# Two landing tiles for each expert weight piece, one buffer for the split down weights, and another order of the splits

## The reference, cut to what matters

```
dest = ...                      # tokens sorted by expert, in blocks of 128 rows
def expert_block(args):
    xblk, e = args              # xblk: 128 x 1024
    hid = jax.nn.silu(xblk @ w_gate[e]) * (xblk @ w_up[e])     # 1024 x 256 each
    return hid @ w_down[e]                                     # 256 x 1024
yb = lax.map(expert_block, (xb, block_e))
```

## Time and profile before

| | us |
|---|---|
| median of 3 runs | 3005.43 (3005.19 to 3011.29) |
| the profiled execution | 3002.1 |
| its span | 3000.5 |
| PE busy in the span | 2580.1 (86%) |
| DVE busy | 1809.9 (60%) |
| ACT busy | 1250.2 (42%) |
| POOL busy | 657.2 (22%) |

### The profile page before, as it was taken

The page is one execution under the profiler, slowest core; times in us unless marked ns, Lnnn a source line. Parts: engine busy times, 40 slices in busy tenths (PEclk is TensorE's granted clock), DMA queues, the critical chain, the costliest instruction groups (busy, mean ns, idle before and its releaser), DMA issues. The chain is left out here.

```text
span 3000.5 us, 42077 instructions
## 1 busy us (share of the span) xinstructions
PE 2580.1 (86%) x12607; PEld 2079.5 (69%) x12608; DVE 1809.9 (60%) x2274; ACT 1250.2 (42%) x1486; POOL 657.2 (22%) x718
## 2 busy tenths in 40 slices
PE   7989998998998999979977843998989989998956
PEld 6778777777877877747856732777777767776832
DVE  3346887787788655537445714566656676566427
ACT  3343453454245333335221102566656665556400
POOL 2012112221212111100002073233323323223200
PEclk9999999999999999989988966999999999999978
DMA  5323233221322232164543135677778797779367
GB/s 120 63 46 68 57 49 59 58 56 50 78 57 50 65 80 75 60 207 138 164 149 102 55 85 178 241 278 276 248 264 280 278 319 261 258 260 326 132 264 316
DMA packets 246835, 462.84 MB, mean 154 GB/s; under 512 B 27144, under 2 KB 151560, under 8 KB 244686
## 3 DMA queue, kind: packets, MB, share of 16 engines
q1 hardware_dynamic: 211870, 377.44, 41.2%
q0 software_dynamic: 34864, 84.04, 7.5%
HBM read 401.02 MB, written 94.40 MB: 165 GB/s over the span
## 5 line engine op out<-in xcount | busy, mean ns | idle before, releaser
L59 PE MATMUL dn_pj<-x_hi,dn_hi 128*128 128x512 f32 x1024 | 439.6, 429 | 3.1 <-PEq L84 1.8
L61 PE MATMUL dn_pj<-x_hi,dn_lo 128*128 128x512 f32 x1024 | 411.7, 402 | 0.0
L60 PE MATMUL dn_pj<-x_lo,dn_hi 128*128 128x512 f32 x1024 | 410.7, 401 | 0.0
L1008 DVE SCALAR_TENSOR_TENSOR uc_half<-u_in,par,uc_half 128x512 f32<-128x512 f32 x480 | 383.3, 799 | 13.1
L2303 ACT ACTIVATE e_hi<-e_raw 128x2048 f32 (+1 forms) x128 | 244.7, 1913 | 244.2 <-DMA e_raw<-in_w_up_e_dram 244.2
L2363 DVE TENSOR_TENSOR e_lo<-e_raw,e_hi 128x2048 f32 (+1 forms) x128 | 290.4, 2287 | 51.5 <-ACT e_hi L2303 51.2
L59 PE MATMUL gu_ps<-e_hi,xg_hi 128*128 (+1 forms) x752 | 310.4, 413 | 0.0
L2200 POOL DMA_INDIRECT y_rows<-y_block,idx_scatter x98 | 160.5, 1637 | 626.0 <-ACT y_block L2322 514.0
L61 PE MATMUL gu_ps<-e_hi,xg_lo 128*128 (+1 forms) x752 | 294.3, 391 | 0.0
L60 PE MATMUL gu_ps<-e_lo,xg_hi 128*128 (+1 forms) x752 | 293.5, 390 | 0.0
L1147 POOL TENSOR_TENSOR a_lvl<-a_t,lvl_mask 128x512 f32<-128x512 f32 x112 | 167.8, 1515 | 352.2 <-PE dn_a L686 223.5
(11 more groups left out here) (374 smaller groups left out, 5010.7 us busy)
## 6 DMA issues: line engine op xcount, KB each, us to landing
e_raw<-in_w_gate_e_dram SPq DMA_DIRECT2D x128, 512.0 KB
e_raw<-in_w_up_e_dram SPq DMA_DIRECT2D x128, 512.0 KB
e_raw<-in_w_down_e_dram SPq DMA_DIRECT2D x128, 512.0 KB
dn_raw<-in_w_in_dram SPq DMA_DIRECT2D x64, 512.0 KB
y_rows<-y_rows SPq DMA_DIRECT2D x8, 2560.0 KB, 31.5
y_rows<-y_rows SPq DMA_DIRECT2D x8, 1536.0 KB, 26.2
gate_rows<-qkv_next SPq DMA_DIRECT2D x16, 512.0 KB, 3.2
br_raw<-in_w_oa_dram SPq DMA_DIRECT2D x16, 512.0 KB
```

The costliest lines, as they stand in the source:

```text
L59: nc.tensor.matmul(out, w_hi, x_hi, start=first, stop=False)
L60: nc.tensor.matmul(out, w_hi, x_lo, start=False, stop=False)
L61: return nc.tensor.matmul(out, w_lo, x_hi, start=False, stop=last)
L1008: ins = stt(out=uc[:], in0=u_in[:, t:t + HALF], scalar=w, in1=uc[:], op0=ALU.mult, op1=ALU.add)
```

## The change

Each landing tile gets a second half, taken by the parity of the expert. The load of expert e into a half waits until expert e-2's piece has been read. Because the two halves share one arrival semaphore, SP also waits until the previous expert's piece has arrived before it issues the next. SP's order becomes gate/up of e+2, then down of e. The split down weights get one buffer in place of two. In an expert's first block ScalarE makes the high part of the down weights last, after the output copy, and VectorE the low part last; VectorE makes the low part of hidden first and puts gate/up piece 0 of e+2 ahead of the product.

```
@@ -2067,11 +2067,11 @@
         with ExitStack() as ctx:
             GU = 2
             BUFS = 3
-            raw = [sb(ctx, f"e_raw{i}", [P, 2, 4 * FF]) for i in range(GU + 1)]
+            raw = [sb(ctx, f"e_raw{i}", [P, 2, 2, 4 * FF]) for i in range(GU + 1)]
             wh = sb(ctx, "e_hi", [P, BUFS, KT, 2, FF], F32R)
             wl = sb(ctx, "e_lo", [P, BUFS, KT, 2, FF], F32R)
-            dh = sb(ctx, "ed_hi", [P, 2, 2, D], F32R)
-            dl = sb(ctx, "ed_lo", [P, 2, 2, D], F32R)
+            dh = sb(ctx, "ed_hi", [P, 2, D], F32R)
+            dl = sb(ctx, "ed_lo", [P, 2, D], F32R)
             xg = [sb(ctx, f"x_gather{s}", [P, D]) for s in range(2)]
             xh = sb(ctx, "xg_hi", [P, 2, KT, P], F32R)
             xl = sb(ctx, "xg_lo", [P, 2, KT, P], F32R)
@@ -2112,8 +2112,8 @@
                         j = e % BUFS
                         x = w[:, j] if isinstance(j, int) else w[:, bass.ds(j, 1)].rearrange("p o k w f -> p (o k) w f")
                         return x[:, 4 * i:4 * i + 4, :, :].rearrange("p k w f -> p w k f")
-                    return raw[i][:].rearrange("p w (k f) -> p w k f", k=4), wkf(wh), wkf(wl)
-                return raw[i][:], of(dh, odd(e)), of(dl, odd(e))
+                    return of(raw[i], odd(e)).rearrange("p w (k f) -> p w k f", k=4), wkf(wh), wkf(wl)
+                return of(raw[i], odd(e)), dh[:], dl[:]
 
             def plan(eng, e):
 
@@ -2143,30 +2143,45 @@
 
             @block.sync
             def _(sp):
-                def load_gate_up(e, first):
+                def arrived(e, i):
+                    if not isinstance(e, int) or e > 0:
+                        sp.wait_ge(w_in[i], e * 32)
+                        alone(sp, self.passed)
+
+                def into(e, i, n):
+                    return of(raw[i], odd(e))[:, n, :]
+
+                def load_gate_up(e):
 
                     for i in range(GU):
-                        if not first:
-                            sp.wait_ge(lo_s, e * GU + (i + 1 - GU))
+                        arrived(e, i)
+                        if not isinstance(e, int) or e >= 2:
+                            sp.wait_ge(lo_s, e * GU + (i + 1 - 2 * GU))
+                        alone(sp, self.passed)
                         for n, w in enumerate((a["w_gate_e"], a["w_up_e"])):
                             src = w[0, bass.ds(e, 1)].rearrange("o (p k) f -> p (o k) f", k=KT)[:, 4 * i:4 * i + 4, :]
-                            sp.dma_start(raw[i][:, n, :].rearrange("p (k f) -> p k f", k=4), src).then_inc(w_in[i], 16)
-
-                def load_down(e, first):
-
-                    if not first:
-                        sp.wait_ge(dlo_s, e)
+                            sp.dma_start(into(e, i, n).rearrange("p (k f) -> p k f", k=4), src).then_inc(w_in[i], 16)
+
+                def load_down(e):
+
+                    arrived(e, GU)
+                    if not isinstance(e, int) or e >= 2:
+                        sp.wait_ge(dlo_s, e - 1)
+                    alone(sp, self.passed)
                     for n in range(2):
                         src = a["w_down_e"][0, bass.ds(e, 1)].rearrange("o (c p) n -> p (o c) n", p=P)[:, n, :]
-                        sp.dma_start(raw[GU][:, n, :], src).then_inc(w_in[GU], 16)
-
-                load_gate_up(0, True)
-                load_down(0, True)
-                load_gate_up(1, False)
-                with sp.Fori(2, E) as e:
-                    load_gate_up(e, False)
-                    load_down(e - 1, False)
-                load_down(E - 1, False)
+                        sp.dma_start(into(e, GU, n), src).then_inc(w_in[GU], 16)
+
+                load_gate_up(0)
+                load_gate_up(1)
+                for e in range(2):
+                    load_gate_up(e + 2)
+                    load_down(e)
+                with sp.Fori(2, E - 2) as e:
+                    load_gate_up(e + 2)
+                    load_down(e)
+                for e in range(E - 2, E):
+                    load_down(e)
 
             @block.gpsimd
             def _(pool):
@@ -2245,11 +2260,10 @@
                         last = nc.tensor.transpose(ht[:, s, h, :], hid[:, s, h * P:(h + 1) * P], self.ident[:])
                     last.then_inc(ht_done, 1)
 
-                def down(e, s):
-                    j = odd(e)
+                def down(s):
                     for h in range(2):
                         for hf in range(2):
-                            w = lambda x: x[:, bass.ds(j, 1), h, hf * HALF:(hf + 1) * HALF].rearrange("p o b -> p (o b)")
+                            w = lambda x: x[:, h, hf * HALF:(hf + 1) * HALF]
                             last = split3(nc, yp[:, hf, :], hh[:, s, h, :], hl[:, s, h, :], w(dh), w(dl), h == 0, h == 1)
                     last.then_inc(y_done, 1)
 
@@ -2272,7 +2286,7 @@
                         pe.wait_ge(hl_s, n)
                         pe.wait_ge(dlo_s, e_prev + 1)
                         pe.wait_ge(y_ready, n + LAG - 1)
-                        down(e_prev, 1 - s)
+                        down(1 - s)
 
                 pe.wait_ge(xg_in[0], 32)
                 transposes(0)
@@ -2290,7 +2304,7 @@
                 pe.wait_ge(hl_s, half * 2)
                 pe.wait_ge(dlo_s, E)
                 pe.wait_ge(y_ready, half * 2 + LAG - 1)
-                down(E - 1, 1)
+                down(1)
 
             @block.scalar
             def _(act):
@@ -2329,8 +2343,6 @@
                     x_hi(n + 1, 1)
                     if prev:
                         hid_hi(n - 1)
-                    if first:
-                        hi(e, GU)
                     if ahead:
                         hi(e + 2, 0)
                     activation(n)
@@ -2338,6 +2350,8 @@
                         hi(e + 2, 1)
                     if prev:
                         y_move(n - 1)
+                    if first:
+                        hi(e, GU)
 
                 for i in range(GU):
                     hi(0, i)
@@ -2384,16 +2398,17 @@
                 def blk(e, n, first):
                     known = isinstance(e, int)
                     ahead = first and (not known or e + 2 < E)
+                    if not first or not known or e > 0:
+                        hid_lo(n - 1)
                     x_lo(n + 1, 0)
                     x_lo(n + 1, 1)
-                    if not first or not known or e > 0:
-                        hid_lo(n - 1)
+                    if ahead:
+                        lo(e + 2, 0)
+                    product(n)
+                    if ahead:
+                        lo(e + 2, 1)
                     if first:
                         lo(e, GU)
-                    product(n)
-                    if ahead:
-                        lo(e + 2, 0)
-                        lo(e + 2, 1)
 
                 for i in range(GU):
                     lo(0, i)
```

## The result

The changed kernel takes 2894.89 us (median of 4 runs, 2892.55 to 2895.82) against 3005.31 (3003.93 to 3011.29) for the kernel before: ratio 0.9628, interval 0.9611 to 0.9644. It is 110 us faster.

A forecast was written before the change was run, and what follows sets the result against it. It took late expert weights, reaching TensorE through ScalarE and `hid_lo`, as the bound. Gains of 68.8 + 21.4 = 90.2 us, less 22 given back, made 68: median 2937 us, 8-in-10 range 2900 to 2990.

The forecast's parts named there:

- What bounded the kernel: Expert-block stage: 107.7 us over TensorE's pace, 68.8 waiting for `hid_lo`, 17.5 on "issue", 21.4 from the clock.
- So this term is kept, not gained.: Loop iteration start: TensorE's 17.5 us wait on "issue" before the transposes stays, 0 to 18 us gained.
- The floor: Expert-block stage: TensorE's own pace of 9.505 us per block, 884.0 us for 93 periods.
- Loop's start: Start of each two-block iteration: 4.17 us from `hid_lo`'s end to the next matmul remains, 18 us in 36 pairs.
- DMA rate: Two long runs of one-block experts: DMA falls short, giving back 10 us (0 to 20).
- Scatter and clock: Output copy's wait for a scatter, now ahead of `ed_hi`: 5 us given back (0 to 20); clock: 5 us.
- `hid_lo` where the 0.9 us is not enough: VectorE before the down product: where the 0.9 us to spare does not suffice, 2 us given back.
- B: Rival, chance 0.22: DMA is the bound; 35 single-block experts keep 2 us each, 38 us go, 2967 us.
- D: Rival, chance 0.08: SP's order and arrival waits delay the down piece, `ed_hi` waits, 64 us lost, 3001 to 3005.
- C: Rival, slower at chance 0.08: GpSimd's scatter chain takes over; 2944 us at 10.0 us per scatter, 3037 at 11.0.
- a tighter packing makes every such scatter a long one: GpSimd behind the output copy: every first-block scatter becomes long, the 10.0 us case, 2944 instead of 2937.
- better than 2915: Whole kernel: a time under 2915 us, below the forecast band of 2915 to 2958, chance 0.10.

The follow-up runs named there:

- e8: The kernel before, with each weight load from expert 1 on bringing a quarter of its bytes: 2900.82 us, ratio 0.9676.
- e5: The changed kernel with one landing tile per piece instead of two, SP's new order kept: 2951.96 us, ratio 0.9844.
- e9: The changed kernel with TensorE alone addressing the down buffer through a register (always 0): 2927.4 us, ratio 0.9744.
- e4: The changed kernel with each weight load from expert 2 on bringing a quarter of its bytes: 2894.01 us, ratio 0.9659.
- e10: The changed kernel with ScalarE and VectorE, not TensorE, addressing the split down buffer through a register (always 0): 2906.42 us, ratio 0.9659.
- e7: The changed kernel with ScalarE making the high part of the down weights before the output copy, still behind its wait: 2870.69 us, ratio 0.957.
- e1: The kernel before with the new ScalarE/VectorE order and single down buffer, but one landing tile and SP's old order: 3387.54 us, ratio 1.1305.

## Why the prediction was right or wrong

**What bounded the kernel: right.** Late weights, through ScalarE, `hid_hi` and `hid_lo`, to TensorE: e8 puts 97 us on them, beside my 90.2 (68.8 + 21.4), and e5 shows that two tiles are what removes them.

**The step that failed: "So this term is kept, not gained."** I took the 4.17 us from `hid_lo`'s end to the next iteration for a constant of the loop. It was that of the `down` of before, whose operands' addresses come from the expert's parity. The diff removes `j = odd(e)` from it, and I read this edit only for its semaphores ("The down buffer adds no semaphore wait"). The runs showed in its place that 0.9 of the 4.17 us were TensorE's register work, and went with it (3.25 left): e9 puts the register work back, on TensorE alone, and the wait (25.4 us in 36 places) and 35 us of time come back.

**The floor was not a floor.** The same error once more: 9.505 us was read from four blocks where nothing was late, and those blocks held the loop's start too. In the trace of before, the iteration that starts at 2523.04:

```profile
2518.47 0.42 DVE L2376 TENSOR_TENSOR hid_lo<-ht_ps,hid_hi  x1 [0.60 <-ACT hid_hi L2313]
...
2523.04 1.15 PE L2232 MATMUL xg_ps<-ident,x_gather 128*128 128x128 f32 x8
```

4.15 us from the end of `hid_lo`, so the register work was in the pace. A pace read from the kernel itself is a floor only for what the change leaves alone. It hid 884.0 - 865.8 = 18.2 us of gain (18.1 before rounding).

**The sum of the miss.** The forecast left 18.1 (in the floor) + 17.5 (loop's start) + 22 (given back) = 57.6 us of excess over 865.8; there are 20.7. By terms:

- Loop's start, in both its guises: 18.1 + 17.5 = 35.6 us forecast, which is what e8 has too. In the changed kernel TensorE's row on "issue" is 0.3 us; the blocks that are not at a one-block expert's boundary have 2 to 5 us of excess left between them, by how the stage's ends are counted. This is nearly the whole miss of 37 us in the stage.
- DMA rate: 10 forecast, none measured. The long single run moved more than my full share of 350 GB/s: 357 [busy row above], and e4 gains nothing from a quarter of the bytes. I had bounded it at 0 to 20, and 0 was the right end.
- Scatter and clock: 5 and 5 forecast, none. ScalarE's wait for a scatter has the same total, 42.3 for 42.0 us, in 29 smaller pieces for 12, longest 2.3 instead of 6.4; it fits in ScalarE's idle time. The clock is 1.00.
- `hid_lo` where the 0.9 us is not enough: 2 forecast, about 18 there. The instruction durations did add up to a fit, "with 0.7 us over"; what I left out is that VectorE's sequencer needs 1.77 us and two register loads between an expert's block and the next expert's, and can begin only when `ed_lo` is issued. With loads of 0.61 us that would have been harmless; most of the 18 us are loads that took up to 1.89. The prediction said that this slack was thin and that below it every late us reaches TensorE; it put 2 us on it all the same. How much of the 1.77 us is the parity index of the landing tiles was not tried; the index of the down buffer, added, made 0 to 9 us by the times and about 5 by the trace (e10).

So two errors stood against each other: too little gain by some 53 us in five terms, and too much by 16 in one. The rest of the 42 us between the forecast median and the measured one is 1.9 us outside the stage, and the 3.3 us that I added to come from a profiled execution to a median: in the changed kernel these two agree (2895.0 and 2894.89).

**The rivals.** B, DMA as the bound, fell: 0.81 over the stage, and e4. D, arrival waits hold the down piece back: fell, no wait of `ed_hi` for its piece is in the list. C, the scatter chain as the bound, fell; the mechanism beside it did not. The scatter's row on the page, before and after (busy us, mean ns, idle us):

```profile
L2200 POOL DMA_INDIRECT y_rows<-y_block,idx_scatter x98 | 160.5, 1637 | 626.0 <-ACT y_block L2322 514.0
```

```profile
L2215 POOL DMA_INDIRECT y_rows<-y_block,idx_scatter x98 | 119.1, 1215 | 462.4 <-ACT y_block L2336 357.3
```

A scatter takes 1.22 us instead of 1.64. What makes one long can be read off the traces. The long scatter of rows 11 (2661.55, 2.55 us) began while VectorE was in the second of these two `e_lo`:

```profile
2658.74 4.49 DVE L2363 TENSOR_TENSOR e_lo<-e_raw,e_hi 128x2048 f32 x2
```

And at the boundary shown of the changed kernel:

```profile
2037.53 2.28 DVE L2377 TENSOR_TENSOR e_lo<-e_raw,e_hi  x1
...
2039.51 1.18 POOL L2215 DMA_INDIRECT y_rows<-y_block,idx_scatter  x1 [5.95 <-ACT y_block L2336]
2040.69 2.33 POOL L2194 COPY idx_gather<-tok_tab 128x1 uint32 x1
```

In the kernel before, 62 of the 98 scatters began while an `e_lo` or `ed_lo` was under way, and each of them ended 0.87 us after that instruction did; the other 36 took 1.00 us. In the changed kernel 60 began so, with the same 0.87 us, but later in the VectorE instruction: they take 1.35 us in the mean instead of 2.01. The copy behind them, `idx_gather`, now meets `ed_lo` in 60 places and ends with it, 2.14 us in the mean instead of 0.20. So the rule that the prediction took from the Trainium skill (SBUF — State Buffer, "Who interferes with whom"), that the two exclude each other, is what the traces show; what failed is the prediction's own step that a tighter packing makes every such scatter a long one (1.0 us more). The wait moved to the copy, where it costs nothing that shows: TensorE waits for a gather once in the stage, at its start. Where a scatter waited for the one before, it is 9.8 us from issue to issue in the mean of 20 and 11.3 at most, after 9.3 and 10.7 before, so that part of C came; GpSimd's wait for its own scatters is still only 96.6 us (111.4 before), and the chain is not the bound at 9.53 us nor at 9.3, as e7 shows.

**The range.** Its low end took the loop term as 0 to 18 gained, but not the floor; with both it would have reached 2882. The chance of 0.10 for better than 2915 was too small for a sum in which the term kept had been explained by nothing but its own value.

## What to carry to other kernels

Read a diff for addresses as well as for semaphores: where an operand's address stops depending on a loop variable, its register instructions go from the queue of the engine that uses it, and ahead of a loop's branch that stands behind a late wait, as here, they are on the path. Don't take the pace of an undisturbed stretch for a floor until it is clear what of it the change touches. Where a schedule is to fit by the sum of its instructions, look at the sequencer's own rows at loop and branch boundaries, its register loads above all, and start the long instruction ahead of the boundary early, as e7 does with a few lines: the sequencer begins on the boundary when that instruction is issued. Whether two engines hold each other up is not told by the mean of an instruction before and after: lay the two engines' rows side by side.

## What the runs showed of the hardware

- 16 more register instructions in TensorE's program, all in the down products, lengthened the way from `hid_lo`'s end to the next iteration's first matmul from 3.25 to 4.12 us, and the time by 35 us in 47 iterations (e9). Inside an iteration they cost little: 40 of 46 blocks there take 9.42 to 9.45 us in e9, and 35 of 46 take 9.31 to 9.49 in the changed kernel.
- A register load from a table in on-chip memory (TENSOR_LOAD in a sequencer) took 0.28 to 0.32 us as a rule, and up to 1.28 us in the changed kernel. Of 393 there, 36 of the 38 over 0.4 us started within 3 us of a scatter instruction's end.
- A GpSimd instruction that began while VectorE was in a subtraction of two on-chip operands (`e_lo`, `ed_lo`) ended after it: scatters 0.87 us after, 62 of 62 before and 60 of 60 in the changed kernel, a 0.20 us copy right with it, 60 of 60. VectorE's own instructions kept their 2.28 to 2.29 us.
- The DMA rate in the run of one-block experts, with loads of 512 KB and indirect gathers and scatters beside them; 2341 to 2401 of the changed kernel:

```profile
DMA packets 6316, 21.15 MB, mean 353 GB/s; under 512 B 1153, under 2 KB 1153, under 8 KB 6316
```

- A wait in an in-order DMA queue can cost more than what it guards: e1 and e5 differ in the order of SP's loads alone, and by 439 us.
